# Dense share of the value rows raised from 1024 to 1152 columns in a two-block layer kernel

## The reference

```python
q = (xn @ wq)                       # 8 heads; two halves of each query are scored against 128 keys each
idx, gate = top16(...), softmax     # 128 rows of the tables per token, with a weight each
u = U[idx]                          # (tokens, 8, 16, 2048)
h = gelu(einsum('thkd,td->thk', u, xb))
w = gate * h
y = einsum('thk,thkd->td', w, V[idx])
h = h + y
```

## Time and profile before

| what | value |
|---|---|
| median of 3 runs | 3580.99 us (3573.34 to 3581.68) |
| profiled execution, its own time | 3580.99 us |
| its span | 3579.2 us |
| mean granted clock of TensorE | 0.983 |
| TensorE matmul busy | 3447.2 us (96% of the span) |
| VectorE busy | 2177.3 us (61%) |
| GpSimd busy | 1007.6 us (28%) |
| ScalarE busy | 635.5 us (18%) |
| bytes moved by DMA | 793.38 MB |

### The profile page before, as it was taken

One profiled execution on the slowest core, in us unless ns is written; L12 is line 12 of the kernel. 1 busy time (PEld: TensorE's weight loads), 2 busy tenths in 40 slices (PEclk: granted clock), 3 DMA queues, 4 the chain that ended last, 5 costly groups with the idle time before them and its releaser, 6 DMA issues. The chain is left out here.

```text
span 3579.2 us, 50054 instructions
## 1 busy us (share of the span) xinstructions
PE 3447.2 (96%) x20178; PEld 3037.7 (85%) x20178; DVE 2177.3 (61%) x4178; ACT 635.5 (18%) x1425; POOL 1007.6 (28%) x797
## 2 busy tenths in 40 slices
PE   8999999999999999999899999991999999999999
PEld 7878878899998888888888766661899999999988
DVE  5883102145555499966798666568366767666653
ACT  0002202100001212222367100001221222222100
POOL 0000100010000055655686677675100112122000
PEclk9999999999999999999999999995999999999999
DMA  5433432244464689999996899999334322222352
GB/s 222 142 133 138 150 132 84 105 169 173 166 232 169 247 301 402 402 409 408 342 333 249 321 409 409 409 402 342 142 141 153 117 91 89 101 101 72 153 201 105
DMA packets 175972, 793.38 MB, mean 222 GB/s; under 512 B 19541, under 2 KB 21485, under 8 KB 140029
## 3 DMA queue, kind: packets, MB, share of 16 engines
q1 hardware_dynamic: 101112, 501.75, 37.5%
q0 software_dynamic: 73728, 285.25, 20.8%
q10 hardware_dynamic: 900, 3.17, 0.3%
HBM read 779.44 MB, written 10.64 MB: 221 GB/s over the span
## 5 line engine op out<-in xcount | busy, mean ns | idle before, releaser
L424 PE MATMUL PS<-mem,ring 128*128 128x272 f32 (+1 forms) x2816 | 648.1, 393 | 1.2 <-DVE mem L938 1.2
L424 PEld LDWEIGHTS PS<-mem,ring 128*128 128x128 f32 x2816 | 542.1, 193 | 105.7 <-issue 6.8
L1334 POOL DMA_INDIRECT mem<-in_peer_ug,idx x256 | 340.9, 1332 | 543.3 <-DVE idx L1949 335.7
L2086 DVE SCALAR_TENSOR_TENSOR mem<-mem 128x1024 f32<-128x1024 f32 x256 | 328.8, 1284 | 174.3 <-DMA mem<-in_peer_vg,idx 169.4
L1363 POOL DMA_INDIRECT mem<-in_peer_vg,idx x256 | 352.3, 1376 | 165.7 <-DVE mem L2086 87.6
L2002 DVE CUSTOM_DVE_ANT_0 mem<-mem 128x1152 f32<-128x1152 f32 x256 | 348.0, 1361 | 78.0 <-DMA mem<-in_peer_ug,idx 77.9
L1475 PE MATMUL PS<-mem 128*128 128x256 f32 x1792 | 387.5, 379 | 0.4 <-DMA mem<-in_peer_ud 0.3
L1475 PEld LDWEIGHTS PS<-mem 128*128 128x128 f32 x1792 | 340.2, 190 | 47.3 <-DMA mem<-in_peer_ud 1.2
L432 PEld LDWEIGHTS PS<-mem,ring 128*128 128x128 f32 x3136 | 350.3, 192 | 0.1
L432 PE MATMUL PS<-mem,ring 128*128 128x128 f32 x3136 | 350.3, 275 | 0.0
L2432 PE MATMUL PS<-mem,ring 128*128 128x128 f32 x2560 | 312.3, 275 | 0.9 <-issue 0.6
(11 more groups left out here) (439 smaller groups left out, 4480.7 us busy)
## 6 DMA issues: line engine op xcount, KB each, us to landing
ring<-in_first_tiles SPq DMA_DIRECT2D x143, 1024.0 KB, 4.8
ring<-in_dn_tiles SPq DMA_DIRECT2D x88, 1024.0 KB, 4.9
mem<-in_peer_vd SPq DMA_DIRECT2D x128, 512.0 KB
mem<-in_peer_ud SPq DMA_DIRECT2D x128, 448.0 KB
ring<-in_out_panels SPq DMA_DIRECT2D x16, 2048.0 KB, 9.6
ring<-in_w_out SPq DMA_DIRECT2D x8, 2048.0 KB, 11.6
ring<-in_peer_wq SPq DMA_DIRECT2D x8, 2048.0 KB, 9.8
mem<-second_keys SPq DMA_DIRECT2D x64, 256.0 KB
```

The costliest lines, as they stand in the source:

```text
L424: last = nc.tensor.matmul(PS[:, 4 + n % 4, 0:T if wide else TX], wslots[slot_of[n]][:, k, :], x, start=(k == 0), stop=(k == KT - 1))
L1334: nc.gpsimd.indirect_dma_start(ugs[at % US], None, a["peer_ug"], bass.IndirectOffsetOnAxis(ap=idx[:, n, j:j + 1], axis=0)).then_inc(u_in[a ...
L2086: nc.vector.scalar_tensor_tensor(hc, vgs[at % GS], dots[:, m, h * PTOP + j:h * PTOP + j + 1], hc, ALU.mult, ALU.add).then_inc(vg_used, 1)
```

## The change

CD becomes 1152, so the gathers bring 896 columns in place of 1024, and the dense product makes 1152 in place of 1024. The loop in `dense` gets a third piece of 128 columns, with a bank of its own (4 for m = 0, 5 for m = 1). `add_dense` adds the two full banks in one instruction of 1024 columns and the third bank in one of 128. Waits and their counts stay as they were.

```diff
-CD = 1024
+CD = 1152
...
                         for at in range(0, CD, BANK):
-                            to = PS[:, 2 * m + at // BANK, :]
-                            last = nc.tensor.matmul(to, weights_of[m][:, i // LO, :, i % LO], vds[i % VS][:, at:at + BANK],
+                            w = min(BANK, CD - at)
+                            to = PS[:, 2 * m + at // BANK, :] if w == BANK else PS[:, 4 + m, 0:w]
+                            last = nc.tensor.matmul(to, weights_of[m][:, i // LO, :, i % LO], vds[i % VS][:, at:at + w],
                                                     start=(i == 0), stop=(i == NKEY - 1))
...
                     def add_dense(m):
                         dve.wait_ge(y_dense, m + 1)
-                        hc = h_tok[:, m, 0:BANK]
-                        nc.vector.tensor_tensor(hc, hc, PS[:, 2 * m, :], ALU.add).then_inc(y_added, 1)
-                        hc = h_tok[:, m, BANK:CD]
-                        nc.vector.tensor_tensor(hc, hc, PS[:, 2 * m + 1, :], ALU.add).then_inc(y_added, 1)
+                        hc = h_tok[:, m, 0:2 * BANK]
+                        nc.vector.tensor_tensor(hc, hc, PS[:, 2 * m:2 * m + 2, :].rearrange("p b n -> p (b n)"),
+                                                ALU.add).then_inc(y_added, 1)
+                        hc, w = h_tok[:, m, 2 * BANK:CD], CD - 2 * BANK
+                        nc.vector.tensor_tensor(hc, hc, PS[:, 4 + m, 0:w], ALU.add).then_inc(y_added, 1)
                         dve.wait_ge(y_added, 2 * m + 2)
```

## The result

The changed kernel takes 3616.64 us (median of 4 runs, 3615.73 to 3623.68), the kernel before 3578.64 us (3573.34 to 3581.68). The ratio is 1.0112 with a 95% interval of 1.0094 to 1.0131: slower by 1.1%. The forecast was 3618 us, in a range of 3600 to 3630 us. The profiled execution of the changed kernel has a span of 3613.2 us.

What follows compares the result with a forecast made beforehand. The later of TensorE's dense chain and the gather chain, meeting at `add_dense(1)`, was taken to bound the stage. Dense passes move it +37.7 us, less 0.8: 3580.99 + 36.9 = 3618 us, range 3600 to 3630 us.

Steps and rivals of the forecast that it cites:

- The bound: At `add_dense(1)`: dense chain ready at 2418.8 us, gather chain at 2491.9 us; TensorE has 73 us to spend free.
- The gather chain: Gathers on the DMA engines: the last ends between 2422 and 2471 us, so this chain is not the later one.
- Both effects that the prediction named: On the DMA engines: lighter gathers lose at least 20.7 us; slower TensorE takes dense loads more slowly, leaving them room.
- The price of a pass: TensorE's dense loop: each new 128-column pass costs 0.217 us for its strided load; dense chain ends at 2529.5 us.
- below 0.144 us a pass: TensorE's 512 new passes: the price per pass that decides between gain and loss.
- The end of the stage: `add_dense(1)` starts at 2529.6 us, 37.7 us later; with 0.8 us less behind it, +36.9 us.
- the 0.8 us of squares: From `add_dense(1)` to the square root of line 1798: 4.2 us in place of 5.0, as only two sums remain.
- The loads of the next stage's weights: SyncE's queue behind the last gathers: start near 2523 us, done about 2536 us, used at 2551 us, no cost.
- The reload is hidden: Rival, 128-column passes: 0.112 us each, dense end 2476.1 us, 3564.5 us in all; chance 0.07.
- One of the two: Rival, one of each matmul's two reloads is hidden: 84.2 us of dense work, 3591 us in all; chance 0.04.
- the whole record: Rival, strided load exposed for its full 0.295 us: 151 us of dense work, 3658 us in all; chance 0.03.

Runs made afterwards that it cites:

- experiment 1: Kernel before (gathers still 1024 wide) with only a third matmul of 128 columns added to each dense step, result unused: 3616.43 us, ratio 1.0100.
- experiment 2: Changed kernel without its third matmul, gathers 896 wide, a ninth of the dense product left out: 3554.80 us, ratio 0.9928 to the kernel before.
- experiment 3: Changed kernel with the 1152 columns cut into 3 x 384 in place of 512 + 512 + 128: 3561.03 us, ratio 0.9946 to the kernel before.
- experiment 4: Changed kernel with contiguous stationary weights (LO = 1 in place of 16), pieces still 512 + 512 + 128: 3603.63 us, ratio 1.0064 to the kernel before.
- experiment 5: Changed kernel with the 1152 columns cut into 448 + 448 + 256: 3566.49 us (one run).
- Experiment 6: Changed kernel with the 1152 columns cut into 480 + 480 + 192: 3589.97 us (one run).
- experiment 7: Changed kernel with LO = 2, stationary values 8 bytes apart in place of 64, pieces 512 + 512 + 128: 3565.97 us (one run).
- experiment 8: Changed kernel with LO = 4, stationary values 16 bytes apart in place of 64, pieces 512 + 512 + 128: 3624.58 us (one run).

## Why the prediction was right

**The bound.** That two chains meet at `add_dense(1)`, with 73 us between them, is shown by experiments 1 and 2: the added dense work alone makes TensorE the later chain (+35 us), the lighter gathers alone leave the gather chain the later one (-26 us), and the two don't add up to the change's +38 us, since only the later chain counts.

**The gather chain.** It was put between 2422 and 2471 us. At 2424.3 us all but its last three steps were done, near the lower end. Both effects that the prediction named are there: between 1985 and 2409 us 202 gathers were taken in before, 224 with the slower TensorE alone (experiment 1), 220 with narrower rows alone (experiment 2) and 240 with both. The width of that range cost the forecast nothing, since this chain was not the later one.

**The price of a pass.** This was the step on which all hung, and it held: 512 passes at 0.217 us, less 0.4, made 110.7 us; the dense stretch grew by 576.8 - 466.5 = 110.3 us. It had been read from four places of the trace where the same load stood behind a pass of the same length. Each of them had one such spot, and that a third matmul would have two of them was argued; the step of 2.15 us shows it. Experiments 3 to 8 show the reason from each side: a longer pass beside the load takes the cost away, and so does a layout that puts two values in 16 bytes. The change would have paid below 0.144 us a pass: in experiments 3, 5 and 7 the dense stretch grew by 56 to 60 us, 0.110 to 0.116 us for each of the 512 passes more, and they took less time than the kernel before. The formula of the Trainium skill ("TensorE: Matmul & The Clock Gate", section "LDWEIGHTS (loading the stationary operand)"), columns / 1.2 ns, has no term for the layout. Here one is needed: with the same 128 columns the records of experiments 4, 7 and 8 are 190, 196 and 309 ns.

**The end of the stage.** Forecast was +37.7 us at `add_dense(1)`, it was 2525.07 - 2491.92 = +33.2 us. The missing 4 us lie ahead of the stage: the first dense matmul came at 1948.3 in place of 1952.3 us, and measured from there `add_dense(1)` moved by +37.2 us. In the other kernels that have LO = 16 that matmul came between 1947.9 and 1956.4 us, so this is how executions differ. From `add_dense(1)` to the next stage it took 2536.25 - 2525.07 = 11.2 us, before 12.05: the 0.8 us of squares that were out of the way (from `add_dense(1)` to the square root 4.1 us, before 5.0). The loads of the next stage's weights had been put near 2523 us. The first went out at 2504.0 us, as soon as SyncE's queue had issued the last dense load, and the other four from 2518.7 us on, behind the last gathers. The first use at 2548.5 us did not wait for them. VectorE's instruction of 896 columns took 1152 ns, where 1124 had been estimated; neither set the time.

**How close the number is.** The medians moved by +38.0 us, and +36.9 was forecast; the two profiled executions differ by 33.9 us. Runs of either kernel differ by up to 8 us, so that 3618 us came within 2 us of the median is in part luck. What is borne out is the working: the step of 2.15 us, the dense stretch and the chain that ends last.

**The rivals.** "The reload is hidden" was worked out at 3564.5 us. With pieces or a layout that hide it, experiments 3, 5 and 7 gave 3561, 3566 and 3566 us, so its working was right, as far as these kernels stand for it, and only its condition was not met. "One of the two" and "the whole record" are out by the step of 2.15 us; they would have made 1.72 + 0.33 = 2.05 and 1.72 + 0.59 = 2.31 us. Experiment 6 happens to have the dense stretch of the first of them, 84.1 us longer than before, and took 3589.97 us, where 3591 us had been worked out.

## What to carry to other kernels

Before you give an engine with slack more work, price that work in the form in which it comes. 128 columns more cost 56 us when all 1152 were cut into three even pieces and 110 us as a matmul of their own, and the slack was 73. When work is cut into pieces, make each long enough to cover the load of the next weights, which an even cut does first; full banks and a small rest were the dearest of the four cuts tried. And look in the trace for a place where the very pair of instructions that a change brings already stands side by side: the row of 0.70 us behind a short pass was worth more here than any average.

## What the runs showed of the hardware that was not expected

- At the distances tried, the cost of a strided stationary operand is a step, not a slope: records of 190 ns contiguous, 196 ns at 8 bytes, 309 ns at 16 bytes, 298 ns at 64 bytes.
- The moving operand has such a cost too: 256 passes of 128 columns take 61.3 us with values 512 bytes apart, against 33.8 us with 16 contiguous ones (experiments 4 and 2); with pairs (LO = 2) it is 34.7 us.
- So has ScalarE's write: its copies of 128 columns out of PSUM into `weights_of[1]` take 427 ns each with values 64 bytes apart and 451 ns at 16 bytes, but 284 ns at 8 bytes and 272 ns contiguous. ScalarE is idle for over 300 us of that stage, so nothing came of it.
- A TensorE that is quicker than its share of the DMA engines waits for its loads even when its buffers are five deep: in experiment 2 it asked for 172 GB/s of the 407 that were moved, and its dense stretch became 23.8 us longer.
